# Order of high and low products in the feed-forward up steps of a two-block transformer kernel

## What is computed

```python
def swiglu(hn, w_in, w_out):             # first block, hidden width 2816
    gate, up = jnp.split(hn @ w_in, 2, axis=-1)
    return (jax.nn.silu(gate) * up) @ w_out

def swiglu_ffn(x, w1, w2):               # second block, D_FF = 2816
    a, b = jnp.split(x @ w1, 2, axis=-1)
    return (jax.nn.silu(a) * b) @ w2
```

## Time and profile before

| | |
|---|---|
| median of 3 runs | 1881.88 us (1881.71 to 1881.93) |
| profiled execution | 1882.02 us |
| its span | 1880.2 us |
| TensorE matmuls busy | 1863.6 us, 99% |
| TensorE weight loads busy | 1601.1 us, 85% |
| VectorE busy | 1340.4 us, 71% |
| ScalarE busy | 861.0 us, 46% |
| GpSimd busy | 124.3 us, 7% |
| read from HBM | 341.20 MB, 182 GB/s over the span |

### The profile page before, as it was taken

The page is one execution under the profiler, slowest core; times in us unless marked ns, Lnnn a source line. Parts: engine busy times, 40 slices in busy tenths (PEclk is TensorE's granted clock), DMA queues, the critical chain, the costliest instruction groups (busy, mean ns, idle before and its releaser), DMA issues.

```text
span 1880.2 us, 28201 instructions
## 1 busy us (share of the span) xinstructions
PE 1863.6 (99%) x10664; PEld 1601.1 (85%) x10664; DVE 1340.4 (71%) x1697; ACT 861.0 (46%) x1107; POOL 124.3 (7%) x155
## 2 busy tenths in 40 slices
PE   9999999999999999999999999999999999999998
PEld 8998888888888888888977888888888897788887
DVE  5676767776767776776876677677777767677777
ACT  5554434474334444344375433443335337644333
POOL 1001200230000100000300100010000020000000
PEclk9999999999999999999999999999999999999999
DMA  7423555425555565544434465556554444455453
GB/s 307 180 90 148 199 181 187 171 82 203 212 191 188 224 223 200 181 167 169 178 137 162 175 227 184 201 218 229 197 182 175 164 166 168 147 189 213 180 199 113
DMA packets 48548, 343.46 MB, mean 183 GB/s; under 512 B 5472, under 2 KB 5504, under 8 KB 8784
## 3 DMA queue, kind: packets, MB, share of 16 engines
q1 hardware_dynamic: 43200, 310.92, 45.5%
q0 software_dynamic: 5264, 31.35, 4.4%
HBM read 341.20 MB, written 1.05 MB: 182 GB/s over the span
## 4 chain that ended last, share of the span: by engine, by line
PE 66%; issue 0%; DVE 0%; POOL 0%; ACT 0%; DVEq 0%; POOLq 0%
PE bank L1068 16%; PE bank L856 12%; PE bank L858 12%; PE bank L857 12%; PE bank L1067 7%; PE bank L919 2%; PE bank L1070 1%; PE bank L1147 1%; PE bank L1519 1%; PE bank L964 1%; PE bank L959 1%; PE bank L960 1%; PE bank L1443 0%; PE bank L1381 0%; PE bank L1508 0%
## 5 line engine op out<-in xcount | busy, mean ns | idle before, releaser
L2065 DVE TENSOR_TENSOR wlo<-raw,whi 128x2048 fp32r<-128x2048 f32 x292 | 672.1, 2304 | 223.2 <-ACT whi L1586 222.7
L1586 ACT ACTIVATE whi<-raw 128x2048 fp32r<-128x2048 f32 x293 | 559.3, 1910 | 256.4 <-PE bank L858 252.3
L1068 PE MATMUL bank<-ysp,whi 128*128 128x512 f32 x1920 | 666.1, 396 | 0.0
L1067 PE MATMUL bank<-ysp,wlo 128*128 128x256 f32 x1680 | 468.6, 279 | 0.0
L1068 PEld LDWEIGHTS bank<-ysp,whi 128*128 128x128 f32 x1920 | 347.7, 188 | 67.0
L1067 PEld LDWEIGHTS bank<-ysp,wlo 128*128 128x128 f32 x1680 | 316.8, 189 | 10.7
L1669 ACT ACTIVATE sg<-sg 128x256 f32<-128x256 f32 x120 | 50.2, 418 | 468.2 <-DVE sg L2262 468.2
L856 PE MATMUL bank<-whi,ysp 128*128 128x512 f32 (+3 forms) x592 | 217.3, 367 | 0.3 <-DVE wlo L2065 0.3
L858 PE MATMUL bank<-whi,ysp 128*128 128x512 f32 (+3 forms) x592 | 212.8, 359 | 0.0
L857 PE MATMUL bank<-wlo,ysp 128*128 128x512 f32 (+3 forms) x592 | 212.4, 359 | 0.0
L856 PE MATMUL bank<-whi,hl 128*128 128x512 f32 x528 | 206.0, 390 | 0.0
(11 more groups left out here) (359 smaller groups left out, 2356.7 us busy)
## 6 DMA issues: line engine op xcount, KB each, us to landing
raw<-stream SPq DMA_DIRECT2D x294, 1024.0 KB, 4.8
sr<-side POOLq DMA_DIRECT2D x10, 1024.0 KB, 5.2
gbc<-gains POOLq DMA_DIRECT2D x11, 512.0 KB, 3.9
cw<-small POOLq DMA_DIRECT2D x2, 2048.0 KB, 10.7
gbias<-gate_rows POOLq DMA_DIRECT2D x6, 512.0 KB, 4.3
dbias<-dilb POOLq DMA_DIRECT2D x1, 2304.0 KB, 12.8
lng<-rows POOLq DMA_DIRECT2D x2, 1024.0 KB, 5.2
tab<-second POOLq DMA_DIRECT2D x1, 1724.0 KB, 15.0
```

The costliest lines, as they stand in the source:

```text
L1067: pe.matmul(o[:, 0, :], lo[:, k, cols], yh[:, k, :], start=False, stop=False, skip_group_check=True)
L1068: last = pe.matmul(o, hi[:, k, cols], ysp[:, :, k, :], start=k == 0, stop=k == 7)
L1586: act.activation(whi[s], raw[s], ACT.Copy).then_inc(hi_made, 1)
L2065: dve.tensor_tensor(wlo[s], raw[s], whi[s].bitcast(F32), ALU.subtract).then_inc(lo_made, 1)
```

## The change

For each of the eight row blocks the high product is now issued first and the low one behind it, for k = 0 as for the others. The last matmul of a block, and so the one that raises `step_done` at the end of the step, is the low product of k = 7. The set of matmuls, their operands and banks are unchanged. The first write to a bank is still the high product of k = 0, which starts the accumulation.

```diff
                     for c in range(2):
-                        o = bank2(up_banks[bank][c])
+                        o, cols = bank2(up_banks[bank][c]), slice(c * P, c * P + P)
                         for k in range(8):
-                            cols = slice(c * P, c * P + P)
-                            if k:
-                                pe.matmul(o[:, 0, :], lo[:, k, cols], yh[:, k, :], start=False, stop=False, skip_group_check=True)
-                            last = pe.matmul(o, hi[:, k, cols], ysp[:, :, k, :], start=k == 0, stop=k == 7)
-                            if k == 0:
-                                pe.matmul(o[:, 0, :], lo[:, k, cols], yh[:, k, :], start=False, stop=False, skip_group_check=True)
+                            pe.matmul(o, hi[:, k, cols], ysp[:, :, k, :], start=k == 0, stop=False, skip_group_check=True)
+                            last = pe.matmul(o[:, 0, :], lo[:, k, cols], yh[:, k, :], start=False, stop=k == 7, skip_group_check=True)
                     last.then_inc(step_done, 1)
```

## The result

The changed kernel takes 1890.66 us (median of 5, 1890.11 to 1891.05) against 1881.76 us: ratio 1.0048, interval 1.0037 to 1.0059, so slower by 0.5%. The medians stand 8.9 us apart; the spans of the two profiled executions, 1888.4 us against 1880.2, stand 8.2 us apart, and it is these 8.2 us that the traces can account for (the profiled execution is 0.4 us under its median after, and 0.3 above it before).

The account below looks back on a forecast made before the run. TensorE, never waiting, was taken as the bound through distances between matmul starts. Exchange, close and waits 0, long rhythm 60 x 0.102 = +6.1 us: 1881.88 + 6.1 = 1888.0 us; 8-in-10 range 1876.5 to 1889.5.

Parts of the forecast that it names:

- What bounds the kernel: Whole kernel: TensorE, busy 99%, waits for nobody, so time is the sum of distances between consecutive matmul starts.
- The exchange itself costs 0: Up steps: same matmuls and weight loads, each distance paid as often as before, so reordering alone costs 0.
- the third rival: Up steps: distances depend on size alone, or half the blocks stay long; no change, 1881.9 us; chance 0.21, indifferent or mixed.
- One rhythm for all four blocks, and the long one: Two up steps: strict alternation holds 0.353 us a pair throughout, 11.28 to 11.29 us, +6.1 us in all; chance 0.48.
- The sign I read it from: Block entry after a down step: first low distance 0.114 us, taken to show the 0.353 us rhythm already at L0.
- the double low product: L0 then L1 at a block's start: named as possibly what throws the block out of the 512-column matmuls' regular spacing.
- Twelve single steps count as six doubles: Feed-forwards: nine double and two single up steps each, counted as 60 doubles at +0.102 us, +6.1 us.
- a fourth rhythm: Up steps: a rhythm absent from the rows shown would make the prediction wrong; no size given.
- The down step's 5.45 us and all else must stay: Down step behind the up steps: its 5.45 us, the counts and everything else were to remain unchanged.
- The drain is released at the same time: Close of the up step: VectorE's drain released at the same moment to 0.01 us, off the path, cost 0.
- The waits come out: Rival at 120 step closes: waits behind a low product exposed, up to 0.11 us each, up to 13 us; chance 0.06.
- Even throughout: Rival in the up steps: 0.347 us a pair, doubles 11.10 us, 5.0 us faster, 1876.9 us; chance 0.25.

Follow-up runs that it names:

- WRRR: Kernel before, but each two up steps start H L L H H L L H, then strictly low, high; in all feed-forwards 1877.15 us against 1881.97, ratio 0.9975.
- RRRR: Kernel before, but all four blocks of two up steps strictly low, high, in one feed-forward: two up steps 11.304 us, down step 5.489.
- OOAA: Kernel before, but the last two of four up-step blocks strictly high, low, in one feed-forward: two up steps 11.234 us, down step 5.467.
- AZAA: Changed kernel, but the second of four up-step blocks closes low, high, in one feed-forward: two up steps 11.293 us, down step 5.467.

## Why the prediction was right or wrong

- *What bounds the kernel*: right. TensorE waits for nobody in the up and down steps of any run, and the time follows the distances between starts.
- *The exchange itself costs 0*: right as to counts. That the order is indifferent (the third rival) is refuted: the same matmuls give 11.10 to 11.30 us a place. The Trainium skill's formula, by which it would be (TensorE: Matmul & The Clock Gate, section Back-to-back issue gap), doesn't give these distances; the same section says that it is for the isolated matmul and that in a stream the weight loads count too, and here every matmul has a load ahead of it.
- *One rhythm for all four blocks, and the long one*: right. The doubles came out at 11.290 us where 11.28 to 11.29 was forecast, in all 54 places, and this is the main part of the loss: 5.8 us of 8.2 (5.5 forecast for these 54, 6.1 with the single steps). But which rhythm it would be was right by luck. The sign I read it from, a first low distance of 0.114 us, tells nothing: low distances of 112 to 114 and of 117 to 118 ns stand in both rhythms, and the one from 211.25 to 211.37 that I compared it with is 113 ns unrounded. It is the high distance of 241 ns and the low one of 120 behind it that the even rhythm lacks. WRRR enters with the same H 227, L 113 as the change and goes even, so the entry is not yet in the long rhythm at L0. That a strict alternation out of the plain rhythm goes long is now shown by the change and by RRRR, which starts with a low product; that the double low product is what pushes it out is refuted by the same two. My picture of what breaks a rhythm was too simple as well, as OOAA and AZAA show.
- *Twelve single steps count as six doubles*: wrong, by 0.8 us. They start from transposes and not from the plain rhythm; after the change four are long (5.737 to 5.739 us) and eight fast (5.634 to 5.642), and together they gained 0.15 us where 0.6 was to be lost. Four of the fast ones are in a further rhythm, H 230, L 117 in every pair, which costs what the even one costs; the prediction had named a fourth rhythm as a sign of being wrong.
- *"The down step's 5.45 us and all else must stay"*: wrong, and this is the step that put the time outside the range. I put the down step at no change without a reason: I took the plain rhythm for a state that 512-column matmuls fall into at once. The trace before gave little warning, as only the first distance of a down step is longer there, 231 ns in place of 227. After the change the first ten distances are 225 to 241 ns, which makes the step behind a double 0.059 us longer, and all down steps together take 3.3 us more. Without these the measured 1890.7 would have been 1887.3, within the range. In the spans the sum is 6.12 forecast, +0.29 in the doubles, +3.35 in the down steps, -0.76 in the single steps and -0.80 for everything else: 8.20 us. Closing high in place of low takes 0.042 us of the 0.059 away (5.461 us).
- *The drain is released at the same time*: right. In both kernels VectorE's reduction behind a double starts 0.20 us after the first start of the down step, 0.43 us after the last high product before and 0.32 us after the last low one now. Nobody on TensorE waits for it.
- *The waits come out*: refuted as a rival. 0.12 us at the close with the wait behind it, in the changed kernel (220.99 to 221.11) and in the kernel before with the close moved.
- *Even throughout*: the mechanism exists and was priced right (11.10 us forecast, 11.096 measured), but this order doesn't lead there.

What stays open: why there is a long and an even rhythm, and which orders lead from one to the other. That the column counts matter and the three operands varied do not is shown. That the rhythms come of the weight loads was only argued: below 256 columns the loads keep 108 and 232 ns whatever the matmuls do, which fits loads that set the 0.34 us of a pair, but no run changed the loads alone. What moved the 0.8 us elsewhere isn't known.

## What to carry to other kernels

Where TensorE never waits, compare distances between starts, block by block, and not durations: a page that says 99% busy can hide a loss, here 0.7% between the slowest and the fastest order of the same matmuls. A stream that alternates long and short matmuls can settle into one of several repeating rhythms, and which one is set by its first products and by what ran ahead of them; so try the order of the first few products, which adds no instruction, and measure. What a stream leaves behind is paid for by the next one, so count the stretch behind a change too.

## What the runs showed that I had not expected

- Several stable rhythms of the same alternation of 512 and 256 columns: 0.347 us a pair (even) and 0.353 (long). Once entered, each holds in every one of its places to the next break, with totals within 3 ns of each other.
- Three double products within the first four row blocks (H L L H H L L H, then strictly alternating) lead from a down step to the fast one, worth 0.087 us a place against before and 4.8 us on the whole kernel.
- Below 256 columns the short product of a pair saves little: 224 columns give 0.343 us a pair with a 512-column partner, 192 and 128 both 0.340.
- The 512-column stream behind an alternation takes from 5.440 to 5.503 us for the same 24 matmuls, by how the alternation was left.
